# Prompt attention by pairs of heads, with the scaling by the reciprocal sum on GpSimd

## What is computed

```python
def sparse_attend(q, kg, vg, q_pos, key_pos, rel_table):
    rel = q_pos[None, :, None] - key_pos
    bias = jnp.swapaxes(rel_table[rel_bucket(rel)], -1, -2)
    logits = (jnp.einsum('bthd,btkhd->bthk', q, kg).astype(jnp.float32) * (HEAD_DIM ** -0.5)
              + bias.astype(jnp.float32))
    logits = jnp.where((rel >= 0)[:, :, None, :], logits, NEG_INF)
    p = jax.nn.softmax(logits, axis=-1).astype(vg.dtype)
    return jnp.einsum('bthk,btkhd->bthd', p, vg)
```

## Time and profile before

| | us |
|---|---|
| median of three runs | 2059.89 (2058.59 to 2072.83) |
| the profiled execution | 2060.33 |
| its span | 2058.5 |
| PE busy | 1774.0 (86%) |
| VectorE busy | 1259.0 (61%) |
| ScalarE busy | 539.6 (26%) |
| GpSimd busy | 503.9 (24%) |

### The profile page before, as it was taken

One profiled execution on the slowest core, in us unless ns is written; L12 is line 12 of the kernel. 1 busy time (PEld: TensorE's weight loads), 2 busy tenths in 40 slices (PEclk: granted clock), 3 DMA queues, 4 the chain that ended last, 5 costly groups with the idle time before them and its releaser, 6 DMA issues.

```text
span 2058.5 us, 28207 instructions
## 1 busy us (share of the span) xinstructions
PE 1774.0 (86%) x10229; PEld 1569.2 (76%) x10229; DVE 1259.0 (61%) x2143; ACT 539.6 (26%) x1118; POOL 503.9 (24%) x278
## 2 busy tenths in 40 slices
PE   6979999978763499999888779999999999999984
PEld 6967898944522256669777679999999999999983
DVE  6368999999996547763462474363453444445466
ACT  6355112112201434430143133022112112202212
POOL 1232332220000101102200225334334334424430
PEclk9999999977876559999987789999999999999996
DMA  7220232215320100003001211111111111111102
GB/s 231 67 67 21 63 90 76 60 29 157 93 82 0 62 0 1 1 11 134 20 11 52 62 42 42 49 45 42 42 42 52 36 48 42 42 42 48 46 14 87
DMA packets 138601, 110.59 MB, mean 54 GB/s; under 512 B 12180, under 2 KB 119948, under 8 KB 138210
## 3 DMA queue, kind: packets, MB, share of 16 engines
q1 hardware_dynamic: 128181, 102.17, 16.5%
q10 hardware_dynamic: 10301, 6.73, 1.1%
HBM read 93.54 MB, written 16.00 MB: 53 GB/s over the span
## 4 chain that ended last, share of the span: by engine, by line
PE 54%; DVE 8%; issue 3%; ACT 2%; DMA 1%; POOL 0%; DVEq 0%; ACTq 0%; SPq 0%; POOLq 0%
PE ps L1573 39%; PE ps L1856 4%; PE ps L1887 4%; PE ps L1565 3%; PE ps L1588 2%; DVE up_conv L1517 1%; DVE n_rstd L1140 1%; DVE n_rstd L1135 1%; DVE up_conv L1516 1%; DMA out_y_prompt<-y_tok 1%; DVE logits L1430 1%; ACT x_probs L1040 1%; PE ps L1960 1%; DVE yT L1144 0%; PE ps L1838 0%
## 5 line engine op out<-in xcount | busy, mean ns | idle before, releaser
L1573 PE MATMUL ps<-h_hi,w_hi 128*128 128x344 f32 x1200 | 385.1, 321 | 8.4 <-DVE xT L1535 4.1
L1573 PE MATMUL ps<-h_lo,w_hi 128*128 128x344 f32 x1200 | 384.0, 320 | 0.0
L1573 PE MATMUL ps<-h_hi,w_lo 128*128 128x344 f32 x1200 | 383.9, 320 | 0.0
L660 POOL TENSOR_SCALAR w_hi<-w_raw 128x1024 fp32r<-128x1024 f32 (+1 forms) x107 | 116.8, 1092 | 1005.0 <-PE ps L1573 506.2
L662 POOL TENSOR_TENSOR w_lo<-w_raw,w_hi 128x1024 fp32r<-128x1024 f32 (+1 forms) x107 | 288.8, 2699 | 8.9
L1573 PEld LDWEIGHTS ps<-h_hi,w_hi 128*128 128x128 f32 x1200 | 225.9, 188 | 10.0 <-DVE xT L1535 5.3
L1535 DVE TENSOR_TENSOR xT<-xT,ps 128x344 f32<-128x344 f32 x264 | 135.3, 513 | 152.4 <-PE ps L1573 149.5
L1573 PEld LDWEIGHTS ps<-h_hi,w_lo 128*128 128x128 f32 x1200 | 226.1, 188 | 0.0
L1573 PEld LDWEIGHTS ps<-h_lo,w_hi 128*128 128x128 f32 x1200 | 225.9, 188 | 0.0
L1516 DVE SCALAR_TENSOR_TENSOR up_conv<-up,fw,up_conv 128x1024 f32<-128x1024 f32 x44 | 62.4, 1418 | 263.1 <-ACT upl L1090 263.1
L1573 PE MATMUL ps<-g_hi,w_hi 128*128 128x344 f32 x528 | 177.6, 336 | 36.1 <-DVE xT L1535 36.1
(11 more groups left out here) (327 smaller groups left out, 3054.0 us busy)
## 6 DMA issues: line engine op xcount, KB each, us to landing
w_raw<-in_w_up SPq DMA_DIRECT2D x44, 512.0 KB, 3.9
w_raw<-in_w_in SPq DMA_DIRECT2D x24, 512.0 KB, 4.2
w_raw<-in_w_down SPq DMA_DIRECT2D x22, 512.0 KB, 3.7
s_k_page<-in_cache_k SPq DMA_DIRECT2D x32, 256.0 KB, 2.8
s_v_pages<-in_cache_v SPq DMA_DIRECT2D x32, 256.0 KB, 3.0
xT<-x_spill SPq DMA_DIRECT2D x1, 4128.0 KB, 13.4
x_tok<-in_x_prompt SPq DMA_DIRECT2D x8, 512.0 KB, 7.5
x_spill<-x_raw SPq DMA_DIRECT2D x16, 256.0 KB, 2.8
```

Of the source, the lines that this page charges most:

```text
L660: pool.tensor_scalar(view(wh), view(wr), 1.0, 0.0, ALU.mult, ALU.add).then_inc(w_hi, 1)
L1573: mm = pe.matmul(out, view(w)[:, k, m0:m0 + m], x(k), start=(k == 0 and q == 0), stop=(k == ktiles - 1 and q == 2))
```

## The change

PE, VectorE and ScalarE go by pairs of heads (`N_PAIRS` = 32) instead of single items. In step j PE does the transposes of pair j - 2, the scores of pair j, then the values of pair j - 2. Scores of an even and an odd head alternate by 512 columns, values by key tile. The even head's transposes go to banks 4 and 5, the odd head's to 7 and 4; the results of every block go to bank 6. VectorE's step is the late copies of pair j - 2, the reciprocals of pair j - 1, the additions of pair j; ScalarE's the copies of pair j - 2, then the exponentials of pair j. The scaling is on GpSimd, between whose instructions the additions for `nb` now stand. There are four buffers `lg`.

```diff
         pool.wait_ge(bt_ok, 1)
...
+        near_bias(2, 0)
+        near_bias(2, 4)
+        for j in range(1, N_PAIRS + 1):
+            for i in (2 * j - 2, 2 * j - 1):
+                b, h = ITEMS[i]
+                row_ = lg[i % 4][:, 0:P * (b + 1)]
+                pool.wait_ge(ri_ok, i + 1)
+                pool.tensor_scalar(row_, row_, ri[:, b % 2, h:h + 1], 0.0, ALU.mult, ALU.add).then_inc(scaled, 1)
+            if j % 4 == 2 and 2 < j // 4 + 1 < NB:
+                near_bias(j // 4 + 1, 0)
+            if j % 4 == 0 and 2 < j // 4 < NB:
+                near_bias(j // 4, 4)
...
+        for j in range(N_PAIRS + 2):
+            if j >= 3 and (j - 3) % 4 == 3:
+                heads_hi((j - 3) // 4)
+            if j >= 2:
+                for n in (2 * j - 4, 2 * j - 3):
+                    k = min(ITEMS[n][0] + 1, 4)
+                    act.wait_ge(t0_t, n + 1)
+                    if n >= 2:
+                        act.wait_ge(pv, 2 * j - 4)
+                    act.activation(pt[n % 2][:, 0:k, :], ps[:, 4 + 3 * (n % 2), 0:k * P].rearrange("p (k n) -> p k n", k=k),
+                                   ACT.Copy).then_inc(t0_c, 1)
+            if j < N_PAIRS:
+                for i in (2 * j, 2 * j + 1):
...
+                    act.activation(row, row, ACT.Exp, bias=mx[:, i % 4, 2:3], scale=DH ** -0.5,
+                                   accum_out=rs[:, b % 2, h:h + 1]).then_inc(exp_ok, 1)
+        heads_hi(NB - 1)
...
-                row_ = lg[n % 3][:, 0:P * (b + 1)]
-                dve.tensor_scalar(row_, row_, ri[:, b % 2, h:h + 1], None, ALU.mult).then_inc(scaled, 1)
...
+        for j in range(N_PAIRS + 2):
+            if j >= 3 and (j - 3) % 4 == 3:
+                heads_lo((j - 3) // 4)
+            if j >= 2 and ITEMS[2 * j - 4][0] >= 4:
+                for n in (2 * j - 4, 2 * j - 3):
+                    k = ITEMS[n][0] + 1 - 4
+                    dve.wait_ge(t1_t, late(n + 1))
+                    dve.wait_ge(pv, 2 * j - 4)
+                    dve.tensor_copy(pt[n % 2][:, 4:4 + k, :], ps[:, 5 - n % 2, 0:k * P].rearrange("p (k n) -> p k n", k=k)).then_inc(t1_c, 1)
+            if 1 <= j < N_PAIRS + 1:
+                for n in (2 * j - 2, 2 * j - 1):
+                    b, h = ITEMS[n]
+                    dve.wait_ge(exp_ok, n + 1)
...
+                    dve.reciprocal(ri[:, b % 2, h:h + 1], rs[:, b % 2, h:h + 1]).then_inc(ri_ok, 1)
+            if j < N_PAIRS:
+                for i in (2 * j, 2 * j + 1):
...
+        for j in range(N_PAIRS + 2):
+            if j >= 2:
+                for n in (2 * j - 4, 2 * j - 3):
+                    b, odd = ITEMS[n][0], n % 2
+                    pe.wait_ge(scaled, n + 1)
+                    if n >= 2:
+                        pe.wait_ge(t0_c, 2 * j - 4)
+                        if late(2 * j - 4):
+                            pe.wait_ge(t1_c, late(2 * j - 4))
+                    for k in range(min(b + 1, 4)):
+                        mm = tr(ps[:, 4 + 3 * odd, k * P:(k + 1) * P], lg[n % 4][:, k * P:(k + 1) * P])
+                    mm.then_inc(t0_t, 1)
+                    if b >= 4:
+                        if odd:
+                            pe.wait_ge(t0_c, n)
+                        for k in range(4, b + 1):
+                            mm = tr(ps[:, 5 - odd, (k - 4) * P:(k - 3) * P], lg[n % 4][:, k * P:(k + 1) * P])
+                        mm.then_inc(t1_t, 1)
+            if j < N_PAIRS:
+                b, h = ITEMS[2 * j]
+                ext = P * (b + 1)
+                if j >= 1:
+                    pe.wait_ge(added, 2 * j)
                 for f in range(0, ext, 512):
                     w = min(512, ext - f)
...
+                    for e in range(2):
+                        lo = 64 * e
+                        mm = pe.matmul(pair(e)[:, f:f + w], qx[lo:lo + DH, h // 2, b * P:(b + 1) * P],
+                                       kT_[lo:lo + DH, h // 2, f:f + w], start=True, stop=True)
...
+            if j >= 2:
+                b, h = ITEMS[2 * j - 4]
...
                 for k in range(b + 1):
...
+                    for e in range(2):
+                        mm = pe.matmul(ps[64 * e:64 * e + DH, 6, h // 2 * P:(h // 2 + 1) * P], v_[:, k, (h + e) * DH:(h + e + 1) * DH],
+                                       pt[e][:, k, :], start=(k == 0), stop=(k == b))
+                mm.then_inc(pv, 2)
```

More of the change, by code:

```diff
@@ L346, in build @@
     pt = [r.take(f"probsT{i}", [P, NB, P]) for i in range(2)]
-    lg.append(r.take("logits2", [P, S]))
-    assert r.at <= rxz.start + mid - 4096
+    lg += [r.take(f"logits{i}", [P, S]) for i in (2, 3)]
+    assert r.at <= rxz.start + mid
     eps = rc.again(rc.at - rc.start).take("eps", [P, 1])
@@ L693, in _, with near_bias @@
         pool.wait_ge(bt_ok, 1)
-        for b in range(2, NB):
+        def near_bias(b, h0):
             near = sc[:, IDX_AT[b] + P * (b - 1):IDX_AT[b] + P * (b + 1)]
[L696 to L701, removed]
+            if b > 2:
+                pool.wait_ge(added, NH * b + h0 - 4)
+            heads = slice(h0, h0 + 4)
+            pool.tensor_tensor(nb[:, heads, :], bt[:, heads, :], near.unsqueeze(1).to_broadcast([P, 4, 2 * P]),
+                               ALU.add).then_inc(nb_ok, 1)
+        near_bias(2, 0)
[10 more added lines that the diff above has]
+                near_bias(j // 4, 4)
         for j in range(SLOT_O + 2, SLOT_CO):
@@ L999, in _ @@
             act.activation(hh[:, CT + m, :], lh[m % 2][:, :], ACT.Copy).then_inc(ln_hi, 1)
[L1001 to L1022, removed]
@@ L1396, in _ @@
         ln_low(CT - 1)
[L1398 to L1428, removed]
-                row_ = lg[n % 3][:, 0:P * (b + 1)]
-                dve.tensor_scalar(row_, row_, ri[:, b % 2, h:h + 1], None, ALU.mult).then_inc(scaled, 1)
[L1431 to L1434, removed]
-                dve.wait_ge(pv, n - 1)
-                dve.tensor_copy(pt[n % 2][:, 4:4 + k, :], ps[:, 5, 0:k * P].rearrange("p (k n) -> p k n", k=k)).then_inc(t1_c, 1)
-            if i >= 13 and (i - 13) % 8 == 0:
-                b = (i - 13) // 8
-                dve.wait_ge(aT_hi, b + 1)
-                dve.tensor_tensor(hl[:, 0:CT, b * P:(b + 1) * P], ps[:, 6 + b % 2, :].rearrange("p (m n) -> p m n", m=CT),
-                                  hh[:, 0:CT, b * P:(b + 1) * P].bitcast(F32), ALU.subtract).then_inc(aT_lo, 1)
@@ L1886, in _ @@
+            if j >= 2:
+                b, h = ITEMS[2 * j - 4]
+                if j == 2:
+                    pe.wait_ge(v_in, 16)
+                pe.wait_ge(t0_c, 2 * j - 2)
+                if b >= 4:
+                    pe.wait_ge(t1_c, late(2 * j - 2))
+                if h == 0 and b >= 1:
+                    pe.wait_ge(aT_hi, b)
+                    pe.wait_ge(aT_lo, b)
                 for k in range(b + 1):
-                    mm = pe.matmul(ps[half:half + DH, 6 + b % 2, h // 2 * P:(h // 2 + 1) * P], v_[:, k, h * DH:(h + 1) * DH],
-                                   pt[n % 2][:, k, :], start=(k == 0), stop=(k == b))
```

78 lines of the change are left out of this document (40 added, 38 removed).

## The result

The changed kernel takes 1990.97 us (median of 4 runs, 1985.88 to 1994.49), the kernel before on the same chip 2059.63 (4 runs): a ratio of 0.965, 95% interval 0.961 to 0.970, so 68.7 us less where 50 were forecast. By the ratio that is 1988 us against a forecast range that began at 1990. The profiled executions stand the same way: 1991.95 against 2060.33, their spans 1990.1 against 2058.5.

What follows compares the result with a forecast made beforehand. The prediction took PE's matmul time as the bound before, the chain over ScalarE's copy in blocks 4 to 7 after. 34 us less in blocks 0 to 3 plus 22, with 6 back, gave 2060.33 - 50 = 2010, range 1990 to 2036.

Steps and rivals of the forecast that it cites:

- Direction and the overlap of the halves: Attention: faster at 0.82; paired scores and values overlap on PE, each 0.225 us per tile and head pair plus fill.
- The chain in blocks 4 to 7: Scores, adds, exponentials, ScalarE's copy, late odd transposes, next scores set steps of 5.4 to 7.5 us; blocks 113, 22 less.
- the milder form of the first rival: First rival: clock stays low through attention, chances 0.07 and 0.03; milder: falls in block 4, 10 us, inside the range.
- The clock I let rise there, in the middle of block 3 as before.: Walk of blocks 0 to 3: low clock until 746.3 us, then two steps at full clock, 3.5 each.
- The walk: Blocks 0 to 3 summed step by step, mostly at the low clock; block 4 starts at 753.3, 34 us less.
- the second rival's case: Clock rises earlier, in block 1 or 2, with shorter steps: 8 to 14 us less, about 1998; chance 0.10.
- the 6 us for unpriced waits: Attention: two or three unpriced PE waits a step, taken as 0.2 us for 32 steps, 6 us added back.
- The bounds named for the upper end: Values not overlapped in blocks 0 to 3, 6; twice the allowance, 6; clock not before block 5, 17: up to 2036.
- The third rival: Score halves don't overlap: chain grows to 6.4 to 9.2 us, about 10 us gained in blocks 1 to 3; 2050, chance 0.06.
- GpSimd: right on the price (1.12 us), half right on the effect.: Scaling on GpSimd in attention: nearest row 1.10 us for 1024 columns; VectorE's scaling is hidden, moving it frees little by itself.

Runs made afterwards that it cites:

- copy_between: The changed kernel with ScalarE's order in a step turned to copy, exponential, copy, exponential instead of both copies, then both exponentials; 1969.16 us, 0.956 of before.
- same_rows_early: The changed kernel with the odd head's scores taken with partitions 0 to 63 too, in blocks 0 to 2 only; 2012.23 us, 0.978 of before.
- copy_between_in_turn: copy_between with the even head's value products ahead of the odd head's, so no column halves stand side by side; 1981.69 us, 0.963 of before.
- values_in_turn: The changed kernel with the even head's value products first, then the odd head's, so no column halves stand side by side; 1991.69 us, 0.967 of before.
- after_warm: The changed kernel plus five extra full-array products of 512 columns on PE at the start of attention, which nothing reads; 1992.17 us, 0.969 of before.
- scores_same_rows: The changed kernel with the odd head's scores taken with partitions 0 to 63 too, in all blocks; 2026.82 us, 0.983 of before.

## Why the prediction fell short

- **Direction and the overlap of the halves: right.** Score halves of a pair were forecast at 2.0 us in block 7 and cost 1.99; values at 0.225 a tile and head pair, and they cost 1.75 for seven tiles and 1.53 for six, 0.22 apart. The Trainium skill (TensorE: Matmul & The Clock Gate, Part 3) would have made the values some 0.27 a tile by an estimate; the trace decides for 0.22. Taken in turn it is 2.89 for seven and 2.46 for six tiles, 0.43 apart.
- **The chain in blocks 4 to 7: right.** Steps were forecast at 5.4, 6.1, 6.8 and 7.5, and are 5.36, 6.05, 6.75 and 7.34 where neither a block's end nor a dip of the clock falls into them. copy_between shows that it was this chain. From block 4's first scores to the last values it is 113.6 us (743.43 to 857.0) against 113. That this is so near is partly luck: the clock's dips, some 4 us, were not in the sum (they are the milder form of the first rival, 10 us there), and the first step of block 4 took 3.48, since the pair that it transposes is still of block 3.
- **The step that failed: "The clock I let rise there, in the middle of block 3 as before."** It rose in block 1, at 715.6. The walk had block 2 at 718.4, block 3 at 735.7 and block 4 at 753.3; they began at 716.85, 729.38 and 743.43. That is 9.9 us, the second rival's case (8 to 14 less), which had been given 0.10. The place of the rise was carried over from the kernel before; no row showed it for the new order. same_rows_early puts the rise back to 743.6 by taking the row halves out of blocks 0 to 2, and the time is 2012. That it comes so near the forecast 2010 is partly chance, since the scores' own time is in it too. Why row halves side by side raise the clock stays open.
- **The term that was too large: the 6 us for unpriced waits.** The steps came out as summed from known rows (5.36 to 7.34 above), without it. The bounds named for the upper end add up to 2039 rather than 2036; nothing hangs on that.
- **Outside attention 2.4 us** went that no step names. That part takes 1128 to 1138 us in the profiles of all these kernels, so it is not put down to the change.
- **Together** 9.9 + 6 + 2.4, less 0.6 in blocks 4 to 7, are 17.7 us, which is 68.4 less 50 but for the rounding.
- **The third rival's price was wrong too.** Scores without overlap were put at 2050 and gave 2027: blocks 0 to 3 took 61.8 us instead of 91.2, so 29 less and not "about 10". The clock rose at 742.7 instead of 777, and there are fewer fills at the low clock; the two were not measured apart.
- **GpSimd: right on the price (1.12 us), half right on the effect.** Moved alone it frees nothing, as the text said; with the pairs it is worth 8 to 12 us, since VectorE's turn comes onto the chain.

## What to carry to other kernels

Where a change alters which part of the array is at work, the place of the clock's rise is a term of its own: work the sum at both levels and weigh them, and do not carry the place over from the kernel before. An overlap under a chain shortens no step until the chain is cut (the column halves here; 12.5 us or more afterwards), so the order of the queue in which the last wait ends, here ScalarE's, is the next thing to try: it gave 22 us with no work changed.

## What the runs showed of the hardware that was not expected

- PE busy in the profile did not go with the granted clock. The old order was at 0.50 for some 70 us while PE was busy 4.00 of 4.00, and fell back to 0.50 within 8 us of being pushed to 1.00; the new order rose to 1.00 where PE was busy 3.61 of 4.00, after 3.91. In all kernels with the pairs' row halves side by side from the start the rise came before 717 us, in the three without them at 742.5 to 743.6, in the old order at 777 to 781. What the chip counts is not shown.
- The clock still dips in the new order where PE waits in each step, in the changed kernel once in block 5 and twice in block 7 (from 770, 831 and 848), 10 us at 0.50 together. In slices of 4 us the first two, and the scores in the second, which take 3.47 instead of 1.99:

```profile
768.00:772.00 4.00, 2.85 (x15) 1.47 (x16) 0.82 (x6) 1.58 (x4) 1.79 (x2) 0.78 0.00 0
...
832.00:836.00 4.00, 4.00 (x30) 1.99 (x28) 1.44 (x6) 0.00 (x0) 2.22 (x2) 0.62 0.00 0
```

```profile
831.28 3.47 PE L1892 MATMUL ps<-kT,qx 64*128 64x512 f32 x8
```

  Neither copy_between nor copy_between_in_turn shows such a dip after the rise, nor does values_in_turn, where PE waits less. An estimate of the cost: the steps with a dip take 7.15, 8.93 and, from the last scores to the output projection, 18.56 us; after_warm, with the same order and no dip in these places, has 6.54, 7.44 and 16.92 there, together 3.7 us less. By this estimate some 4 of the 24.6 us that the turned order gains in attention are the clock. scores_same_rows was at 0.50 for some 24 us after its rise.
